# Four of 24 modulation blocks on VectorE, interleaved unit by unit with TensorE's

## The reference

```
ada = silu(c) @ w_ada[l] + b_ada[l]          # c: (1, 2048), w_ada: (2048, 12288)
sh1, sc1, gt1, sh2, sc2, gt2 = split(ada, 6)  # 2048 each
h = rmsnorm(x, norm1_g) * (1 + sc1) + sh1     # feeds the projection w_in
x = x + gt1 * mix                             # after attention and pooling
h2 = rmsnorm(x, norm2_g) * (1 + sc2) + sh2    # feeds the experts
x = x + gt2 * hier_moe(h2, ...)
```

## Time and profile before

| what | value |
|---|---|
| time, median of 3 runs | 2376.13 us (2370.96 to 2379.33) |
| time of the profiled execution | 2377.56 us |
| its span | 2375.3 us |
| PE busy | 2087.5 us (88%) |
| PEld busy | 1354.4 us (57%) |
| DVE busy | 1257.6 us (53%) |
| ACT busy | 858.0 us (36%) |
| read from HBM | 691.66 MB, mean 293 GB/s |

### The profile page before, as it was taken

How to read it: one execution, slowest core, us unless ns; L and a number is a source line. 1 busy time by engine, 2 the same in 40 slices (tenths; PEclk the granted TensorE clock), 3 DMA queues, 4 the chain that set the end, 5 groups by cost and what they waited for, 6 DMA issues and landing times.

```text
span 2375.3 us, 38332 instructions
## 1 busy us (share of the span) xinstructions
PE 2087.5 (88%) x14512; PEld 1354.4 (57%) x14512; DVE 1257.6 (53%) x2281; ACT 858.0 (36%) x1308; POOL 32.6 (1%) x32
## 2 busy tenths in 40 slices
PE   6899999979988888888888888999998999998997
PEld 2687767752222222222222222998888999997887
DVE  3455566454444444444444445558855554477655
ACT  3343344431111111111111113447854544466543
POOL 0000000000000000000000001011100000000000
PEclk9999999999999999999999999999999999999999
DMA  9998977889999999999999999463445355543442
GB/s 364 377 342 297 305 266 260 291 318 367 422 422 422 422 422 422 422 422 422 422 422 422 422 422 392 151 212 123 137 151 169 125 186 182 177 147 100 136 137 93
DMA packets 135046, 695.44 MB, mean 293 GB/s; under 512 B 14992, under 2 KB 15120, under 8 KB 85264
## 3 DMA queue, kind: packets, MB, share of 16 engines
q1 hardware_dynamic: 134928, 693.81, 76.9%
HBM read 691.66 MB, written 2.10 MB: 292 GB/s over the span
## 4 chain that ended last, share of the span: by engine, by line
PE 48%; DMA 34%; DVE 9%; ACT 4%; issue 2%; SPq 2%; DVEq 0%; ACTq 0%
PE acc L1171 33%; DMA ring<-in_w 30%; DMA land<-in_stream_a 3%; PE psO L1223 3%; PE psS L1447 3%; PE acc L1168 3%; DVE WL L1914 2%; ACT WH L1606 1%; SPq L1032 1%; DMA land<-in_stream_bc 1%; PE psM L1433 1%; PE acc L1433 1%; ACT SB L1691 1%; PE psT L1107 1%; PE psO L1115 0%
## 5 line engine op out<-in xcount | busy, mean ns | idle before, releaser
L1171 PE MATMUL acc<-HH,WH 128*128 128x256 f32 x2408 | 707.4, 294 | 24.6 <-DVE HL L1940 9.9
L1171 PE MATMUL acc<-HH,WL 128*128 128x256 f32 x2408 | 689.2, 286 | 0.0
L1171 PE MATMUL acc<-HL,WH 128*128 128x256 f32 x2408 | 688.7, 286 | 0.0
L1914 DVE TENSOR_TENSOR WL<-land,WH 128x1024 fp32r<-128x1024 f32 (+2 forms) x346 | 416.3, 1205 | 413.9 <-ACT WH L1606 410.0
L1171 PEld LDWEIGHTS acc<-HH,WH 128*128 128x128 f32 x2408 | 470.1, 195 | 49.9 <-issue 11.6
L1171 PEld LDWEIGHTS acc<-HH,WL 128*128 128x128 f32 x2408 | 470.3, 195 | 1.9 <-issue 1.0
L1171 PEld LDWEIGHTS acc<-HL,WH 128*128 128x128 f32 x2408 | 469.9, 195 | 0.0
L1606 ACT ACTIVATE WH<-land 128x1024 fp32r<-128x1024 f32 (+2 forms) x350 | 362.4, 1037 | 224.6 <-PE acc L1171 179.1
L1447 PE MATMUL psS<-ring,low 128*32 128x512 f32 x2048 | 276.5, 612 | 106.6 <-DMA ring<-in_w 103.5
L1447 PEld LDWEIGHTS psS<-ring,low 128*32 128x32 f32 x2048 | 40.8, 108 | 319.7 <-DMA ring<-in_w 285.1
L1756 ACT ACT_TABLE_LOAD x32 | 41.1, 1283 | 456.8 <-PE psS L1447 456.8
(11 more groups left out here) (357 smaller groups left out, 2107.9 us busy)
## 6 DMA issues: line engine op xcount, KB each, us to landing
ring<-in_w SPq DMA_DIRECT2D x384, 1024.0 KB, 26.5
land<-in_stream_a SPq DMA_DIRECT2D x284, 512.0 KB, 7.4
land<-in_stream_bc SPq DMA_DIRECT2D x246, 512.0 KB, 3.9
land<-in_stream_bc SPq DMA_DIRECT2D x12, 384.0 KB, 3.2
X<-in_xT SPq DMA_DIRECT2D x1, 2048.0 KB, 14.7
out<-low SPq DMA_DIRECT2D x4, 512.0 KB, 2.6
cst<-in_const SPq DMA_DIRECT2D x1, 1538.0 KB, 10.1
low<-in_w_pool SPq DMA_DIRECT2D x1, 1024.0 KB, 8.3
```

The costliest lines, as they stand in the source:

```text
L1171: mm = pe.matmul(bank[:, 0:S], w[:, kk, :], h[:, rows[kk], :], start=(z == 0 and i == 0), stop=stop)
L1914: ins = dve.tensor_tensor(wl, src, wh, ALU.subtract)
```

## The change

Blocks 8, 10, 12 and 14 are computed by VectorE (`ADA_DVE`). A unit of such a block is four instructions over 128x512 elements (one for each 128 rows), each multiplying the landed rows with the matching column of silu(c) and adding to an accumulator in `PTS` (two accumulators, used by turns). After unit 3 the turn of the block on TensorE is four matmuls of the accumulator's 128-column slices with one column of ones, which sum over the partitions. VectorE then adds the bias with one instruction. The copy by ScalarE goes for these blocks.

The list `left` changes its order: the units of an even block alternate with those of the odd block behind it, (8, 0), (9, 0), (8, 1), (9, 1) and so on to (15, 3); then blocks 16 to 23 as before. The positions in the list at which a unit is taken stay the same. The turns move too. Blocks that are complete wait in `whole`, and at unit 1 of a TensorE block all of them are turned, one right behind the other: blocks 8 and 9 ahead of (11, 1), 10 and 11 ahead of (13, 1), 12 and 13 ahead of (15, 1), 14 and 15 ahead of (16, 1). Each turn on TensorE waits for VectorE's part of the turn before it.

```diff
+ADA_DVE = (8, 10, 12, 14)
+ADA_PE = (*ADA_FIRST, *(b for b in range(8, 24) if b not in ADA_DVE))
...
+    def turn():
+        b = whole.pop(0)
         o.add("pe", "adaT", b)
         o.add("dve", "adaT", b)
+    def turn_all():
+        while whole:
+            turn()
     def ada(b, q):
-        if q == 1 and b != ADA_FIRST[0] and ("adaT", ada_before(b)) not in o.at["pe"]:
-            ada_t(ada_before(b))
+        by = "dve" if b in ADA_DVE else "pe"
+        if q == 1 and by == "pe":
+            turn_all()
...
         for h in range(2):
-            o.piece(("ada", b, q), h, HALF, "pe", "ada", b, q)
-        o.add("pe", "ada", b, q)
+            o.piece(("ada", b, q), h, HALF, by, "ada", b, q)
+        o.add(by, "ada", b, q)
         if q == 3:
-            o.add("act", "evac", ("ada", b))
+            if by == "pe":
+                o.add("act", "evac", ("ada", b))
+            whole.append(b)
...
-    left = [(b, q) for b in (*ADA_FIRST[4:], *range(8, 24)) for q in range(4)]
+    left = [(b, q) for b in ADA_FIRST[4:] for q in range(4)]
+    left += [(b + z, q) for b in ADA_DVE for q in range(4) for z in range(2)]
+    left += [(b, q) for b in range(16, 24) for q in range(4)]
...
                     elif what == "adaT":
+                        if b in ADA_DVE:
+                            needs(k, "dve", o, "ada", b, 3)
+                        else:
+                            needs(k, "act", o, "evac", ("ada", b))
+                        if n:
+                            needs(k, "dve", o, "adaT", turns[n - 1])
...
+                            if b in ADA_DVE:
+                                mm = pe.matmul(bank[:, c:c + 1], weighed_rows(b)[:, P * c:P * c + P], ones[:, 0:1],
+                                               start=True, stop=True, skip_group_check=True)
+                            else:
+                                mm = pe.transpose(bank[:, P * c:P * c + P], AD[:, P * c:P * c + P], ident)
...
+                    elif what == "ada":
+                        if q == 0 and n > 1:
+                            needs("pe", "adaT", ADA_DVE[n - 2])
+                        for i, p in enumerate(o.pieces_of["ada", b, q]):
+                            dve.wait_ge(unit_in[k][p % LAND[k]], 16 * (p // LAND[k] + 1))
...
+                                if c == 0:
+                                    ins = dve.tensor_scalar(g, w[:, z, :], cs[:, c:c + 1], None, ALU.mult)
+                                else:
+                                    ins = dve.scalar_tensor_tensor(out=g, in0=w[:, z, :], scalar=cs[:, c:c + 1], in1=g,
+                                                                   op0=ALU.mult, op1=ALU.add)
+                                if (i, z) != (1, 1):
+                                    then(ins)
```

More of the change, by code:

```diff
@@ L369 @@
 ADA_FIRST = (4, 5, 6, 7, 0, 1, 2, 3)
+ADA_DVE = (8, 10, 12, 14)
+ADA_PE = (*ADA_FIRST, *(b for b in range(8, 24) if b not in ADA_DVE))
 def ada_before(b):
-    return b - 1 if b >= 8 and b > 8 else ADA_FIRST[ADA_FIRST.index(b) - 1] if b < 8 else ADA_FIRST[-1]
+    return ADA_PE[ADA_PE.index(b) - 1]
 PAIRS = ("v", "dv")
@@ L461, in between @@
         owed[0] += rate
-        b = ada_before(left[0][0]) if left and left[0][1] == 0 else None
-        if shared[0] and b is not None and ("adaT", b) not in o.at["pe"]:
-            ada_t(b)
+        if shared[0] and whole and left and left[0][1] == 0:
+            turn()
             return
@@ L477, in shifts @@
         elif ("adaT", 3) not in o.at["pe"]:
-            ada_t(3)
+            turn()
             modulate(3)
@@ L527, in order_a @@
     index()
-    assert not idx
-    ada_t(23 - len(left) // 4)
+    assert not idx and left[0][0] >= 16
+    turn_all()
     shared[0], owed[0] = True, 0.0
@@ L566, in order_a @@
             o.add("dve", "shiftW")
-        if not left and ("adaT", 23) not in o.at["pe"]:
-            ada_t(23)
+        if not left and whole:
+            turn_all()
             o.add("dve", "gt2rows")
@@ L931, in qt_of, with weighed_rows @@
             return j[-1] if isinstance(j, tuple) else j // 2
+        def weighed_rows(b):
+            return PTS[:, ADA_DVE.index(b) % 2, :, :].rearrange("p a b -> p (a b)")
         def rot_of(x):
@@ L1099, in attention @@
                         needs(k, "dve", o, *o.early[-1])
-                        needs(k, "dve", o, "adaT", max(s[1] for s in o.steps["pe"][:o.at["pe"][("T", 0)]] if s[0] == "adaT"))
+                        needs(k, "dve", o, "adaT", [s[1] for s in o.steps["pe"][:o.at["pe"][("T", 0)]] if s[0] == "adaT"][-1])
                     needs(k, "dve", o, "scale", j)
@@ L1181, in run @@
                 idx = [s[1] for s in o.steps["pe"] if s[0] == "idx"]
+                turns = [s[1] for s in o.steps["pe"] if s[0] == "adaT"]
                 def bank_of(step):
@@ L1954, in run @@
                         ins = dve.tensor_tensor(a, a, C("b_ada", 4 * b, 4), ALU.add)
+                    elif what == "ada":
+                        _, b, q = step
+                        n = ADA_DVE.index(b)
+                        g = weighed_rows(b)
+                        if q == 0 and n > 1:
+                            needs("pe", "adaT", ADA_DVE[n - 2])
+                        for i, p in enumerate(o.pieces_of["ada", b, q]):
+                            dve.wait_ge(unit_in[k][p % LAND[k]], 16 * (p // LAND[k] + 1))
+                            w = land[k][:, p % LAND[k], :].rearrange("p (c n) -> p c n", c=2)
+                            for z in range(2):
+                                c = 4 * q + 2 * i + z
+                                if c == 0:
[5 more added lines that the diff above has]
+                                    then(ins)
                     elif what == "h1":
```

22 lines of the change are left out of this document (12 added, 10 removed).

## The result

The changed kernel took 2397.87 us in the median of 4 runs (2393.72 to 2407.03), the kernel before 2375.62 us of 4 (2370.96 to 2379.33). The ratio is 1.0097, with a 95% interval of 1.0080 to 1.0114: 22 us slower, where I had forecast 10.5. The time lies just inside the range that I gave (2376 to 2398). The profiled execution of the result's kernel took 2407.03 us and its span 2404.7, which is 9 us above the median; the span before was 2375.3.

A forecast was written before the change was run, and what follows sets the result against it. TensorE was taken to bound the kernel between the k heads and the last q heads. Terms of 0 up to 186 us, +5.0 to the last q head, +5.5 at block 16 and 0 for transfers gave +10.5: 2387 us, range 2376 to 2398.

The forecast's parts named there:

- the handoffs: At (11, 1), (13, 1), (15, 1), TensorE's second turn waits for VectorE's first: 11.2 us in all, bounds 6 and 14.
- The turn with one column: TensorE's turn of a VectorE block, four products with one column: 0.95 us, against 0.53 for a turn before.
- The rotation of kw: Before 186 us, this TensorE step waits for VectorE's rotation of k 1 and comes at 185.35 us, where it was.
- Block 16: Turns of 14 and 15 ahead of (16, 1): TensorE's work no longer lies under its VectorE wait; +5.5 us, bounds 4 and 7.
- the part on the transfers: Landing of pieces for TensorE after VectorE frees slots about 4.4 us later: just fits, 0 us, bounds 0 and 5.
- Up to 186 us: nothing is won: Ahead of the rotation of kw, TensorE's head start is waited away on VectorE: 0 us, bounds -2.5 and +1.
- a sign of being wrong: The prediction is wrong if, among other signs, TensorE waits for landed pieces between 190 and 330 us.
- ScalarE's copies: Behind q-head halves without a unit, small TensorE steps wait for ScalarE's copy: +3.4 us, bounds 0 and 4.
- rival C: Landing buffers: later freed pieces make TensorE's odd units wait, at four of sixteen; +13 us, 2400 us; chance 0.10.
- The clock: After each of the three handoffs TensorE's clock falls to half speed: 1.4 us each, 4.2 in all.
- Rival B: Nothing measurable: idle times near 2 us, clock stays up, some gain before 186 us survives; 2379 us, chance 0.21.
- Rival A: Faster: handoffs cost nothing, or other work covers block 16; 18.4 us won minus 1.5 for turns, 2359 us; chance 0.09.

The follow-up runs named there:

- e6: Changed kernel with only the three middle pairs of turns, at (11, 1), (13, 1) and (15, 1), taken apart; 2381.08 us, ratio to before 1.0028.
- e7: Changed kernel with the 1 MB transfer of w_pool issued later, behind the pieces of qi 1; 2401.04 us, ratio to before 1.0109.
- g1: Changed kernel, no turns side by side, half of VectorE's products and weights left out, w_pool later; 2364.02 us, ratio to before 0.9959.
- e1: Changed kernel with no two turns side by side; 2375.14 us, ratio to before 0.9994.
- h3: The changed kernel measured again, unaltered; 2400.45 us, ratio to before 1.0098.
- f3: Changed kernel with no turns side by side and half of VectorE's products left out, all weights loaded; 2369.23 us, ratio to before 0.9968.
- f2: Changed kernel with no turns side by side and VectorE's units loading half of their weights; 2373.09 us, ratio to before 0.9984.
- h2: Second measurement of: changed kernel, only blocks 10, 12, 14 on VectorE, no turns side by side, w_pool later; 2369.22 us, ratio to before 0.9971.

## Why the prediction was wrong

The direction was right, and the handoffs, which I held to be the main loss, were there as described. The size was not: 10.5 us forecast, 22.3 measured. A second loss that I had priced at nothing was there too.

**What held.** VectorE's product took 752 ns (taken 750) and a unit 3.11 (3.15). The Trainium skill's formula in "VectorE: DVE Perf Modes" gives 691 ns; the trace does not agree for this form. The turn with one column took 0.95, the products at L1241 are fewer by 128 (672 to 544). The handoffs: forecast idle 3.1, 4.4 and 3.7, found 3.56, 3.56 and 4.88, 12.0 against 11.2. The sum is closer than its parts, which missed in both directions: at the second place the rotation and the pooled mean, which I added, stayed hidden (VectorE still waits 2.11 us for ScalarE ahead of that low part), and the third was 1.2 longer. With the clock I had 15.4, and e6 measured 16.8. The rotation of kw was forecast where it had been, since TensorE's head start is used up in VectorE's row; e7, nearly free of the landing wait, has it 0.6 us from there. Block 16: forecast 5.5, found 5.4 in the milestones and 3.6 to 8 in the runs (its 0.7 for three units at the half clock should by its own rows be 3 x 0.88 - 1.4 = 1.2). The wait there, 7.93, was forecast as about 8.

**The step that failed** is the part on the transfers: "It just fits: 0, bounds 0 and 5." The same step took "Up to 186 us: nothing is won", with +1 as its upper bound, out of its bounds. I had found the right numbers: pieces come free 4.4 us later, 6.5 to 7.5 us are left to land, and landing takes 7.0 in the median. Where the median just fits, part of the pieces are late, and I read it as none. In the place of the 0 there were 8.5 us of landing waits (0.7 before the change), 4.76 of them at (9, 1), where the 1 MB of w_pool stood ahead, and 3.2 us of half clock behind two of them. It is also what I had named as a sign of being wrong, a wait for landed pieces between 190 and 330 us: there was one, at 253.85. g1 shows it from the other side.

**A second term was wrong, and hid part of the first.** For ScalarE's copies, which a unit used to cover, I added 3.4 us. I had read it from waits of PEld, and weight loads overlap TensorE's matmuls. The index step on TensorE shows what a q head costs without and with a unit, first before the change (268.50 to 272.88 without, 277.36 to 282.92 with one), then after it (without):

```profile
268.50 0.49 PE L1332 MATMUL psS<-low 64*128 64x128 f32 x4
272.88 0.49 PE L1332 MATMUL psS<-low 64*128 64x128 f32 x4
277.36 0.49 PE L1332 MATMUL psS<-low 64*128 64x128 f32 x4
282.92 0.49 PE L1332 MATMUL psS<-low 64*128 64x128 f32 x4
...
295.49 0.49 PE L1359 MATMUL psS<-low 64*128 64x128 f32 x4
299.87 0.49 PE L1359 MATMUL psS<-low 64*128 64x128 f32 x4
```

That is 4.38 us without and 5.56 with a unit, and 4.38 again after the change: the unit's time is won in full. One wait of 0.8 us for ScalarE is new, at another place (unit (11, 0), at 212.33); a second, of 0.97 at 182.55, is taken up by the rotation waits behind it.

**The sum again, from the profile after.** 10.5, less 2.6 for ScalarE, plus 7.8 of landing waits, 3.2 of half clock behind them, 0.8 and 2.0 for the idle time and the clock of the handoffs, and 0.8 for a wait on VectorE's rotation (at 286.65) gives 22.5, where the milestones have 23.1.

**What I said about rival C.** Its mechanism happened and its 2400 was near, and I gave it 0.10. The argument against it ("TensorE is no faster on the whole, so the rate asked is the same") is about averages. But between two handoffs TensorE is faster, 1.15 us for each two halves, and the waits stand there. e1, where nothing else is lost, has as many.

**The clock.** I forecast 1.4 us behind each handoff; e6 has 16.8 - 12.0 = 4.8 us for three, 1.6 each, and the timeline 6.2 for three. The Trainium skill, in "TensorE: Matmul & The Clock Gate", section "Loop structure matters more than you think", marks a copy out of PSUM by VectorE as something that "doesn't break PE warmth", in a loop whose next matmuls "follow immediately". The kernel before is that case, and its trace agrees: turns with work behind them, clock 1.00. The handoffs are not, since TensorE waits for VectorE, and the clock was 0.50 in the window of 318 us. I should not have read the sentence as one on the handoffs. Rival B needed idle times near 2 us and a clock that stays up, and had neither.

**Rival A** (handoffs cost nothing, 2359) did not occur; e1 shows that even without handoffs the gain does not come.

## What to carry to other kernels

Work that moves to a half idle engine brings its latency to whoever waits for that engine next: look up what stands ahead of each wait in its list, and put one piece of the waiter's own work between the piece handed over and the wait (e1 took 22.7 us off by moving four turns by one unit). A transfer whose median time to land equals the time that is left is late in part of the cases, so "it just fits" is not to be priced at nothing. A wait of the weight loads is a loss only if the matmuls show it too. And a landing wait that is removed where it is longest can come back elsewhere: measure the total, not the place.

## What the runs showed of the hardware

- A short idle time of TensorE does not decide by its length whether the granted clock falls. After idle times of 1.88 and 2.00 us the unit took 1.91 and 1.94 (after, h3); after 2.49 and 1.98 it took 1.06 (f3, f2), after 1.89 1.07 (after), and after only 1.11 us 1.94 (h2). What stood before differs from case to case, and I have not worked it out.
- The products with a scalar from a column took 752 ns with a second tensor operand and 486 ns without one (L2001 and L1999), both 512 elements wide.
